# An expert loop by tiles, an early expert and new filler slots in a two-block transformer kernel

## The reference

```python
logits = (t @ w_router + b_router)
top_val, top_idx = lax.top_k(logits, 4)
probs = softmax(top_val)
# rows sorted by expert; x_rows: the token rows of one expert
gu = xb @ w_gate_up[e] + b_gate_up[e]            # 1024 -> 2048
x_glu = minimum(gu[:, 0::2], 7.0)
x_lin = clip(gu[:, 1::2], -7.0, 7.0)
act = x_glu * sigmoid(1.702 * x_glu) * (x_lin + 1)
y = act @ w_down[e] + b_down[e]                  # 1024 -> 1024
out = sum over the 4 choices of probs * y
```

## Time and profile before

| | us |
|---|---|
| median of three runs | 3326.22 |
| lowest and highest run | 3324.42, 3329.95 |
| the profiled execution, its own time | 3331.52 |
| its span, first to last instruction | 3329.8 |

### The profile page before, as it was taken

One profiled execution on the slowest core, in us unless ns is written; L12 is line 12 of the kernel. 1 busy time (PEld: TensorE's weight loads), 2 busy tenths in 40 slices (PEclk: granted clock), 3 DMA queues, 4 the chain that ended last, 5 costly groups with the idle time before them and its releaser, 6 DMA issues.

```text
span 3329.8 us, 46098 instructions
## 1 busy us (share of the span) xinstructions
PE 3017.5 (91%) x19817; PEld 1561.9 (47%) x19817; DVE 952.9 (29%) x1975; ACT 681.7 (20%) x1408; POOL 188.9 (6%) x180
## 2 busy tenths in 40 slices
PE   6899989999899999889989877699899999999995
PEld 2555434444345666666556655433333333333343
DVE  2244220000122221555445455321121212111223
ACT  0133110000012333344443332111010111111102
POOL 0000000000000000211111111100000000000001
PEclk8999889999999999999999988799899999998997
DMA  3134312211211113311110110598999979999696
GB/s 152 51 124 177 118 51 76 76 63 51 103 36 32 34 45 114 114 45 45 45 45 20 45 39 2 191 418 337 418 373 383 418 310 418 397 380 391 266 391 238
DMA packets 120062, 585.13 MB, mean 176 GB/s; under 512 B 10196, under 2 KB 25716, under 8 KB 73012
## 3 DMA queue, kind: packets, MB, share of 16 engines
q1 hardware_dynamic: 95904, 536.14, 40.6%
q10 hardware_dynamic: 17652, 24.25, 2.0%
q0 software_dynamic: 6304, 21.80, 1.8%
HBM read 551.58 MB, written 30.57 MB: 175 GB/s over the span
## 4 chain that ended last, share of the span: by engine, by line
PE 79%; DMA 9%; DVE 6%; ACT 3%; another core or an unknown queue 1%; issue 1%; ACTq 0%; SPq 0%; POOL 0%; DVEq 0%; POOLq 0%
PE product_banks L874 37%; PE product_banks L1284 14%; PE product_banks L1306 8%; DMA space<-in_wgu 6%; PE score_banks L1178 3%; DMA x<-in_wgu 2%; PE out_bank L1037 1%; PE score_banks L974 1%; PE out_bank L996 1%; PE product_banks L1203 1%; PE turn_bank L947 1%; PE product_banks L861 1%; PE out_bank L957 1%; DMA space<-in_wdn 1%
## 5 line engine op out<-in xcount | busy, mean ns | idle before, releaser
L874 PE MATMUL product_banks<-space 128*128 128x512 f32 (+2 forms) x3888 | 1383.4, 508 | 39.0 <-ACT space L1414 19.4
L874 PEld LDWEIGHTS product_banks<-space 128*128 128x128 f32 x3888 | 686.1, 196 | 614.0 <-issue 547.4
L1284 PE MATMUL product_banks<-space 128*32 128x512 f32 x4864 | 583.8, 614 | 55.3 <-DMA space<-in_wgu 52.4
L1284 PEld LDWEIGHTS product_banks<-space 128*32 128x32 f32 x4864 | 141.7, 111 | 377.0 <-issue 270.4
L1306 PE MATMUL product_banks<-space,rstd 128*32 128x256 f32 x5024 | 301.9, 393 | 1.9 <-DMA space<-in_wdn 0.8
L2085 DVE TENSOR_TENSOR sq<-product_banks,cst 128x512 f32<-128x512 f32 x85 | 58.8, 692 | 748.5 <-PE product_banks L1284 748.5
L1414 ACT ACTIVATE space<-product_banks 128x512 f32<-128x512 f32 (+1 forms) x226 | 109.9, 522 | 767.0 <-PE product_banks L874 745.3
L1306 PEld LDWEIGHTS product_banks<-space,rstd 128*32 128x32 f32 x5024 | 168.4, 114 | 163.1 <-issue 72.1
L787 POOL TENSOR_TENSOR space<-space 128x512 f32<-128x512 f32 x112 | 132.6, 1198 | 999.9 <-ACT space L1566 901.8
L1178 PE MATMUL score_banks<-space 128*128 128x64 f32 x896 | 125.4, 288 | 27.3 <-issue 21.1
L1178 PEld LDWEIGHTS score_banks<-space 128*128 128x128 f32 x896 | 123.8, 211 | 42.2 <-issue 38.3
(11 more groups left out here) (319 smaller groups left out, 2478.4 us busy)
## 6 DMA issues: line engine op xcount, KB each, us to landing
space<-in_wgu SPq DMA_DIRECT2D x232, 1024.0 KB, 21.3
space<-in_wdn SPq DMA_DIRECT2D x116, 1024.0 KB, 22.4
space<-in_wt SPq DMA_DIRECT2D x104, 1024.0 KB, 5.1
x<-in_wgu SPq DMA_DIRECT2D x24, 1024.0 KB, 23.6
y_rows<-zeros ACTq DMA_DIRECT2D x2, 6400.0 KB, 29.3
x<-in_wdn SPq DMA_DIRECT2D x12, 1024.0 KB, 23.2
y_rows<-zeros ACTq DMA_DIRECT2D x84, 128.0 KB
space<-in_wt SPq DMA_DIRECT2D x13, 512.0 KB, 4.5
```

Of the source, the lines that this page charges most:

```text
L874: ins = nc.tensor.matmul(bank[0:rows, at:at + cols], lhsT, rhs, start=(i == 0), stop=(i == len(mm) - 1))
L1284: ins = nc.tensor.matmul(bank[ROWS * g:ROWS * g + ROWS, :], xT_[:, k, :], w[:, 512 * g:512 * g + 512], start=(k == 0), stop=(k == DC - 1))
```

## The change

- `HEAD_SLOTS` becomes exact counts for 19 places: five ahead of the levels, 14 in them, none after the output products. Instead of the last place, two products of the stage after the next are issued there, ahead of the norm sum. The wait for the first direction's state moves into the second direction. `MIX_SLOTS` places the last head's 28 products in the first three places. ACT's drains move with them; its last drain stands before the copy of the outputs.
- At the start ACT evacuates pair 0 ahead of the memory root, and pairs 1 to 3 ahead of the sines.
- Expert 16 always stands at place 0 with two groups. Its 12 tiles are loaded when the heads are done (ten) and when the first mixed products are done (two), into slots that are free by then; the order of the slots in the ring changes for it.
- The groups of an expert are cut into chunks of at most three. In a chunk each up tile is used by all its groups in turn (three banks), and each down tile likewise. PE's order is: transposes of inputs needed by this chunk, down products of the chunk before the last, first half of the up products, transposes of the last chunk's activations, second half. Stores of rows have three buffers.
- The biases of an expert are loaded by SP as four rows each, 32 partitions apart, and DVE spreads them over 32 partitions by one `stream_shuffle`; the selector, its matmuls and ACT's copies are gone. SP waits for the spread of the expert two before.
- The last loop has the same steps for its group, with the bias loaded in it.

The core of the diff:

```diff
...
+YMLA_SLOTS = 3
+SLOT_ORDER = list(range(YMLA_SLOTS, H3_SLOT)) + list(range(YMLA_SLOTS)) + list(range(HR_SLOT + 2, NS_SPACE))
...
+RANKS = [6, 5, 5, 4, 4, 4] + [3] * 8 + [2] * 14 + [1] * 2
+EARLY_EXPERT, EARLY_BLOCKS, EARLY_TILES = N_EXP // 2, 2, 10
+N_FIXED = len(RANKS) + 1
...
+CHUNK = 3
+Chunk = namedtuple("Chunk", "q at n first last")
+
+
+def chunks_of(q):
+    n = BLOCKS_AT[q]
+    m = -(-n // CHUNK)
+    sizes = [n // m + (i < n % m) for i in range(m)]
+    return [Chunk(q, FIRST_AT[q] + sum(sizes[:i]), sizes[i], i == 0, i == m - 1) for i in range(m)]
+
+
+CHUNKS = [c for q in range(N_FIXED) for c in chunks_of(q)]
+N_CHUNKS = len(CHUNKS)
 N_TURNS = N_FIXED_BLOCKS * ROWS // P
+TURNS_BEFORE = [[i for i in range(1, N_TURNS) if c.at <= 4 * i < c.at + c.n] for c in CHUNKS]
...
-        UP = [G[:, 0:512], G[:, 512:1024]]
-        DN = [G[:, 1024:1280], G[:, 1536:1792]]
+        UP = [G[:, 512 * i:512 * i + 512] for i in range(CHUNK)]
+        DN = [G[:, 1536:1792], G[:, 1792:2048], PO[:, 256:512]]
+        TURN = [PT[:, 0:256], PT[:, 256:512], PO[:, 0:256]]
...
-        HEAD_SLOTS = [7, 1, 5, 1] + [1] * 14 + [2]
+        HEAD_SLOTS = [21, 1, 20, 3, 13] + [6, 6, 6, 5, 5, 5, 5] + [2, 2, 2, 2, 2, 3, 3]
+        MIX_SLOTS = [18, 0, 10]
+        assert sum(HEAD_SLOTS) == 7 * 2 * DC and sum(MIX_SLOTS) == 4 * (DC - 1)
...
+                for t in range(MT):
+                    if t == EARLY_TILES:
+                        sp.wait_ge(s_o2, DC)
+                    sp.dma_start(tile_slot(t, t), early_source(t)).then_inc(s_w[t], 16)
...
+                def load_bias(e, to, signal):
+                    heads = to[0:P:ROWS, :]
+                    sp.dma_start(heads[:, 0:512], bgu[bass.ds(e, 1), :].rearrange("a (g n) -> (a g) n", g=4)).then_inc(signal, 16)
+                    sp.dma_start(heads[:, 512:768], bdn[bass.ds(e, 1), :].rearrange("a (g n) -> (a g) n", g=4)).then_inc(signal, 16)
...
                 for q in range(N_FIXED):
                     e = sp.value_load(tab_i[0:1, q:q + 1], min_val=0, max_val=N_EXP - 1)
-                    for t in range(MT):
+                    if q == 0:
+                        sp.wait_ge(s_bzero, 1)
+                    elif q > 1:
+                        sp.wait_ge(s_bc, q - 1)
+                    if q != 1:
+                        load_bias(e, raw_bias[q % 2], s_brow[q % 2])
+                    for t in range(MT if q else 0):
                         g = MT * q + t
-                        if g == H3_SLOT:
+                        if g == H3_AT:
                             sp.wait_ge(s_hst, 16 * TT)
-                        if g == HR_SLOT:
+                        if g == HR_AT:
+                            assert q == 1
+                            sp.wait_ge(s_bzero, 2)
+                            load_bias(e, raw_bias[1], s_brow[1])
                             sp.wait_ge(s_xtp, 1)
-                        if g == NS_SPACE:
+                        if g == X_SLOTS[0]:
                             sp.wait_ge(s_xkept, 16)
...
+                    self.lead(sum(MIX_SLOTS[:i + 1]) - self.done)
...
                 for d in range(2):
                     if n and d == 0:
-                        filler.lead(3)
+                        fillers[n].lead(3)
                         norm_spread(f"head{n - 1}")
...
+                    if d:
+                        pe.wait_ge(s_st, 2 * n + 1)
...
-                    pe.wait_ge(s_st, 2 * n + d + 1)
+                fill(4)
+                pe.wait_ge(s_st, 2 * n + 2)
...
-                        fill(4 + L)
+                        fill(5 + L)
...
-                fill(18)
+                if n < 7:
+                    pe.wait_ge(s_evac, stages[f"hg{n + 1}"][1])
+                    fillers[n + 1].lead(2)
...
-            def expert_bias(n):
-                pe.wait_ge(s_picks, n + 1)
-                pe.wait_ge(s_bc, n)
-                nc.tensor.matmul(PO[:, :], sel, bias_rows[:, 0:512], start=True, stop=True)
-                nc.tensor.matmul(PT[:, 256:512], sel, bias_rows[:, 512:768], start=True, stop=True).then_inc(s_bp, 1)
...
+            def turn_chunk(i):
+                c = CHUNKS[i]
+                pe.wait_ge(s_actr, c.at + c.n)
+                pe.wait_ge(s_atc, i)
+                if c.n == CHUNK:
+                    pe.wait_ge(s_y, c.at)
+                for b in range(c.n):
+                    for half in range(2):
+                        ins = nc.tensor.transpose(TURN[b][:, P * half:P * half + P], actb[b][:, P * half:P * half + P], ident)
+                ins.then_inc(s_atp, 1)
+
+            def up_chunk(i):
+                c = CHUNKS[i]
+                pe.wait_ge(s_xtc, (c.at + c.n - 1) // 4 + 1)
                 for k in range(DC):
-                    if halfway and k == DC // 2:
-                        halfway()
-                    w = tiles[k]
-                    if landed:
-                        pe.wait_ge(*landed(k))
-                    for g in range(4):
-                        ins = nc.tensor.matmul(bank[ROWS * g:ROWS * g + ROWS, :], xT_[:, k, :], w[:, 512 * g:512 * g + 512],
-                                               start=(k == 0), stop=(k == DC - 1))
-                    if k == DC - 1:
-                        ins.then_inc(s_up, 1)
-                    elif last:
+                    if i and k == DC // 2:
+                        turn_chunk(i - 1)
+                    if c.first:
+                        pe.wait_ge(*tile_landed(c.q, k))
+                    for b in range(c.at, c.at + c.n):
+                        if k == 0 and b >= CHUNK:
+                            pe.wait_ge(s_u, b - CHUNK + 1)
...
+                        ins = up_step(UP[b % CHUNK], block_inputs(b), k, slots[(MT * c.q + k) % NS])
+                        if k == DC - 1:
+                            ins.then_inc(s_up, 1)
...
+            def down_chunk(i):
+                c = CHUNKS[i]
+                pe.wait_ge(s_atc, i + 1)
+                if c.at:
+                    pe.wait_ge(s_y, c.at)
                 for d in range(4):
-                    w = v3(tiles[DC + d], 2)
-                    if landed:
-                        pe.wait_ge(*landed(DC + d))
-                    for c in range(2):
-                        for g in range(4):
-                            ins = nc.tensor.matmul(bank[ROWS * g:ROWS * g + ROWS, :], aT_[:, P * c + ROWS * d:P * c + ROWS * d + ROWS],
-                                                   w[:, c, 256 * g:256 * g + 256], start=(d + c == 0), stop=(d + c == 4))
-                    if d == 3:
-                        ins.then_inc(s_dn, 1)
-                    elif last:
+                    if c.first:
+                        pe.wait_ge(*tile_landed(c.q, DC + d))
+                    for b in range(c.n):
+                        ins = down_step(DN[b], aT[b], d, v3(slots[(MT * c.q + DC + d) % NS], 2), b != 1, b != 0 or c.n == 1)
...
+            for i in range(N_CHUNKS):
+                for n in TURNS_BEFORE[i]:
+                    turn_inputs(n)
+                if i >= 2:
+                    down_chunk(i - 2)
+                up_chunk(i)
+            down_chunk(N_CHUNKS - 2)
+            turn_chunk(N_CHUNKS - 1)
+            down_chunk(N_CHUNKS - 1)
...
+            evacuate_to(stages["in1"][0] + 1)
             norm_root("mem")
+            evacuate_to(stages["in1"][0] + 4)
...
-                    if L:
-                        drain(3 + L)
-                drain(17)
+                    drain(4 + L)
+                drain(18)
...
+            for i in range(N_CHUNKS):
+                for n in TURNS_BEFORE[i]:
+                    if n >= 2:
+                        act.wait_ge(s_up, 4 * n - 4)
+                    copy_inputs(n, xTb[n % 2])
+                if i:
+                    sigmoids(i - 1)
+                    copy_chunk(i - 1)
+                if i >= 2:
+                    store_chunk(i - 2)
...
+            def spread_bias(source, to):
+                V.stream_shuffle(to, source, [0] * ROWS).then_inc(s_bc, 1)
...
+            def chunk_rows_out(i):
+                c = CHUNKS[i]
+                dve.wait_ge(s_dn, c.at + c.n)
+                for b in range(c.n):
+                    if c.at + b >= CHUNK:
+                        dve.wait_ge(s_yst[(c.at + b) % CHUNK], 16 * ((c.at + b) // CHUNK))
+                    rows_out(c.at + b, DN[b], biasb[c.q % 2], yb[(c.at + b) % CHUNK])
+
+            for i, c in enumerate(CHUNKS):
+                if c.first:
+                    dve.wait_ge(s_brow[c.q % 2], 32 * (c.q // 2 + 1))
+                    if c.q >= 2:
+                        dve.wait_ge(s_y, FIRST_AT[c.q - 1])
+                    spread_bias(raw_bias[c.q % 2], biasb[c.q % 2])
+                    dve.wait_ge(s_bc, c.q + 1)
+                for b in range(c.n):
+                    gated(c.at + b, UP[(c.at + b) % CHUNK], biasb[c.q % 2], actb[b])
+                if i == 1:
                     dve.wait_ge(s_ycleared, 32)
-                if j:
```

(5 more changed lines are left out.)

273 lines of the change are left out of this document (127 added, 146 removed).

## The result

| | before | after | change |
|---|---|---|---|
| median, us | 3328.1 | 3246.4 | -81.7 |
| ratio, 95% interval | | 0.9749 | 0.9727 to 0.9771 |
| profiled execution, us (span) | 3331.5 (3329.8) | 3236.8 (3235.0) | -94.8 |

A forecast was written before the change was run, and what follows sets the result against it. The prediction took PE's own work, waits and low clock to bound the heads, and PE and DMA, nearly equally loaded and coupled by a 20-tile ring, the expert loop. -16 - 46 - 50 = -112 us from 3326.2 gave 3214, range 3172 to 3270.

The forecast's parts named there:

- Part 1: Start: evacuating the first product pairs earlier on ACT removes 13.1 us of waiting and 3.1 of low clock, -16.2 us.
- Part 2: Heads: earlier norm and new slots save 44 us over six heads; head 0 +3.7, head 7 -6; sum -46 us.
- Rival C: Heads: they give nothing, because ACT ends last in the level loop; 3260 us, chance 0.12.
- Part 3: Expert loop: bias products and low clock gain, the other terms give 0; sum -50 us, bounds -140 and -6.
- Bias products: Expert loop: 43 us of bias products are removed from PE, of which 29 lie on the path, -29 us.
- Low clock: Expert loop: groups sharing tiles leave PE less idle; half of the 43 us lost to low clock returns, -21 us.
- Early tiles: Expert loop: preloading saves 18 us of DMA, 12 become idle, the rest is within the error, 0.
- Start and gather: Loop start: ACT's first input copy may run earlier, -5 us; turning the second inputs lacks cover, +5 us.
- Rival D: Expert loop: it gives nothing, the removed 43 us turn into tile waits; 3264 us, chance 0.08.
- B: Expert loop: it drops to near PE's floor, -115 us instead of -50; 3149 us, chance 0.10.
- E: Expert loop, slower: SP waits for DVE's bias spread, itself behind row stores; +155 us, 3369 us, chance 0.04.
- F: Expert loop, slower: groups alternating in three PSUM banks make PE's clock fall; +84 us, 3348 us, chance 0.02.

The follow-up runs named there:

- slots2: Kernel after with other filler slots in the heads, three more products ahead of the first keys: 3234.8 us, ratio 0.9724.
- old_slots: Kernel after with nearly the old filler slots of the heads, the early norm kept: 3285.9 us, ratio 0.9885.
- thin_bias: Kernel before with the two bias products of each expert from the second on cut to 8 columns each: 3327.9 us, ratio 0.9995.
- bias_work: Kernel after with three unread products of 128x512 added ahead of each expert's first up product: 3259.1 us, ratio 0.9797.
- single: Kernel after with every group a chunk of its own, so no tile is shared by groups: 3264.3 us, ratio 0.9813.
- tiles_late: Kernel after with the twelve early tiles issued only behind the expert table: 3250.1 us, ratio 0.9769.
- half_tiles: Kernel after with only half of each tile transferred from the 21st tile of the fixed experts on: 3114.8 us, ratio 0.9347.
- half_cols: Kernel after with each up product 256 instead of 512 columns wide, all tiles transferred: 3236.2 us, ratio 0.9726.
- bias_on_act: Kernel of the order, with bias rows from the third fixed expert on loaded from ACT's queue instead of SP's: 3226.4 us, ratio 0.9698.
- the order: Kernel slots2 with the fixed experts in another order of sizes: 3226.2 us, ratio 0.9693.

## Why the prediction was right in sign and range, and where its size failed

**Part 1** was right: -16 forecast, -16.9 in the trace, -18 alone.

**Part 2**, -46 forecast, -39 measured (-34.7, +3.0, -7.6). The mechanism was right: keys forecast at 22.5 us after the output products, at 21.8 in the trace; level loop at 46, at 46.5 (1563.60 to 1610.07). Mis-sized was the level loop: it took 36.5 us where I had 34.8, and 1.1 of the difference are two waits for DVE that my sum of products leaves out. That is the missing 1.6 us a head. "PE reaches the keys 2 us early" is what happened, but I booked it as harmless. It is a wait of 2.18 us with 1.7 us of low clock behind it, a gain left lying, which slots2 took for 2.1 us a head net. One emphasis was wrong: I derived the gain from the norm's earlier start; old_slots keeps that and has no gain at all. The early norm brings the keys forward, but it needs the slots to turn this into time. Head 0 (+3.7) was right to a microsecond. Rival C, ACT ending last, is out: PE waits 0.46 and 0.65 us in the levels of a head, both times for DVE.

**Part 3**, -50 forecast, -32 measured, is where the forecast failed, term by term:
- Bias products, -29. This is the wrong step. I read their share off the chain of work as if removing them shortened the chain. thin_bias took 27 of 43 us away and gained nothing; bias_work put 86 us in, and 13 reached the end. A chain tells what the end waited for in this execution, not what comes second; here it was the tile transfers, with nearly the same load.
- Low clock, -21. Sharing is worth 18 us (single), so the size is right, but not by the account that I gave. Against single the clock rises from 0.93 to 0.97, and PE's busy time falls by 40 us, twice what the end gets; the rest turns into waiting. Against before the mean clock only rose from 0.96 to 0.97, 11 us, and the waits for tiles, which I left at 50, rose to 88 with their sister group. Seen from the DMA, sharing loses some 18 us less.
- Early tiles, 0: right within the error, 4 us, and for the reason given (15 of 18 us became time lost; I had 12 of 18).
- Start and gather, -5 and +5: neither came. The loop's first product moved by +0.3 (it stands at 2102.2; my sign of 2140 to 2155 less 62 would have been 2078 to 2093), and the second chunk waits 1.2 us for the second inputs. That the sum is right is luck.
- Last iteration and sums, 0: the last iteration is 5 us longer, outside my +-3, with a wait of 10 us for ACT's copy of its inputs; the sums are within their scatter.
- What single, thin_bias and tiles_late leave unexplained: single is still some 10 us shorter than before in the loop, 3 by early tiles. The other 7 may lie with the bias products, the later down products or the slots' new order; that part wasn't separated.

My own condition, that the forecast is wrong if the DMA's idle time is much below or above 100 us, held: 98. The other signs that I gave for the loop did not: about 1030 us long (1048), a clock of 0.98 (0.97), 40 to 60 us of waits for tiles (88). And I took the whole forecast from PE's side and kept the DMA's side only as a bound. The DMA's side has no term for the bias products, but it doesn't hit the number either: 999 us of transfers less 18, plus the 112 us that before lost, give 1093 us, and with 12 of the 18 coming back 1105, -6, which was my bound. The measured 1081 (-30) lies between it and -50. What was missing there is what sharing saves of the DMA's lost time, and no row of before showed that. Rival D was right about the bias products and wrong about the rest of the loop.

**Rivals.** B (PE's own length) needs less work for the DMA; with half of it, half_tiles gets there.

E is out: stores of rows held DVE for up to 10.4 us and 66 in sum, but SP never waited for a spread of bias rows; only once, at the start, for their buffer to be cleared. That wait is not small: SP stands 25.6 us behind DVE's memset at 2101.9, and the DMA falls from 428 GB/s (2080 to 2085 us) to 120, 0 and 33 in the five-microsecond stretches from 2090 to 2105. It lies ahead of the loop's window, so the losses in the table above don't count it. The DMA falls to 172 GB/s again from 2130 to 2150, so the slots were probably full again by then and it cost little; no run took it out.

F is out: with three banks in turn the clock is 0.97, and 1.00 in half_tiles. The Trainium skill ("TensorE: Matmul & The Clock Gate", section "A second HAM failure mode: psum-queue depth-cycling") has a kernel whose clock went up and down while it cycled through banks; these traces show nothing of the kind. The shuffle takes 1.03 us for each expert on DVE, hidden, between the bounds of 0.55 and 1.76. The Trainium skill ("VectorE: DVE Perf Modes", section "The perf-mode tier table") has about 2400 ns for 2048 elements, from which my estimate was 0.9.

```profile
L2144 DVE STREAM_SHUFFLE cst<-space 128x768 f32<-128x768 f32 x31 | 31.8, 1025 | 0.5 <-issue 0.4
```

**Open.** What the remaining 90 to 98 us of lost transfer time are. They hardly fall with PE's work (half_cols), not with the bias issues moved (bias_on_act), and only by 5 with the order. Late releases are not excluded: in half_cols SP still waited 182 us in all for released tiles (331 in the kernel after), most of it until a down product released one, and those stand a chunk later in any case. An up tile takes 20 us from issue to landing by the profile after; whether a deeper ring, or tiles released sooner, would fill the gaps was not tried.

## What to carry to other kernels

Where two resources with nearly equal loads share a ring, add up each one's own length plus its lost time, and don't book work taken off one side at its share in the chain: here 27 us less gave 0, 288 us less gave 10, 86 us more cost 13. Halving each load in turn measures this in two runs. And a wait of 2 us ahead of matrix products can cost nearly twice its length, because low clock comes on top (2.18 and 1.7 us here; filling it gave back 2.1 net): move filler work there first.

## What the runs showed of the hardware that was not expected

Products with 32 output partitions run beside each other: with two instead of four column groups, 48 instructions took 10.47 us and 96 took 10.48. The Trainium skill ("TensorE: Matmul & The Clock Gate", section "The mechanism") says that tiles of the array can hold different weights and compute on different slices of the output, so that they overlap; this trace agrees. So dropping a group saves nothing, while halving the columns did save.

Around a load of 4 partitions ahead of a tile the DMA's share fell to 0.43 over 4 us in half_cols, and in single microseconds to 0.26 (2463.87 to 2465.87 us), which is 4 of 16 engines. The Trainium skill ("DMA: Bandwidth & Descriptors", section "Why a DMA increments its semaphore by 16 and not by 1") says that the number of engines follows from the outer dimension, 4 here, which would fit. That the tile ahead had been finished by the other twelve is my reading, not shown.

The clock granted in an untouched stretch differs between executions of the same instructions (0.84 in the kernel after and 0.75 in single at 300 to 340 us), enough to move everything behind it by 7 us of 3240: the difference of two profiled executions has to be checked against it before it is given to an edit.
